# Adding attention masks with the row maximum instead of with matrix products

## What is computed

```python
# block 1, heads 0..3 (pairs of maps): causal
s = where(kpos <= qpos, q @ k.T * scale, -inf); p = softmax(s)
pd = p[:, :, 0] - lam * p[:, :, 1]
# block 1, heads 4..7 (pairs): three dilated windows (128,1), (512,4), (2048,16), joined by
# their log-sum-exp, which is one softmax of the scores + log(count of windows that hold the key)
# block 2: forgetting attention (causal, + cum_log_f), latent attention (causal, with rope),
# sliding window with a linear penalty and a sink:
s = where(0 <= dist < 128, q @ k.T * scale - slope * dist, -1e30)
p = softmax(concat(s, sink))
# and stick-breaking attention, with no softmax
```

## Time and profile before

| | |
|---|---|
| median of 3 runs | 2500.44 us (2499.18 to 2501.18) |
| the profiled execution | 2499.24 us |
| its span, first to last instruction | 2497.5 us |
| TensorE products, busy | 2447.4 us, 98% |
| VectorE, busy | 1238.2 us, 50% |
| ScalarE, busy | 953.7 us, 38% |
| mean granted TensorE clock | 0.997 of full |

### The profile page before, as it was taken

How to read it: one execution, slowest core, us unless ns; L and a number is a source line. 1 busy time by engine, 2 the same in 40 slices (tenths; PEclk the granted TensorE clock), 3 DMA queues, 4 the chain that set the end, 5 groups by cost and what they waited for, 6 DMA issues and landing times.

```text
span 2497.5 us, 30086 instructions
## 1 busy us (share of the span) xinstructions
PE 2447.4 (98%) x11932; PEld 1953.0 (78%) x11932; DVE 1238.2 (50%) x2019; ACT 953.7 (38%) x1765; POOL 0.2 (0%) x4
## 2 busy tenths in 40 slices
PE   8999999999999999999999999999999999999998
PEld 6888778887888778887767688888886767888887
DVE  6677553345577663344454463333355445433334
ACT  5355432223345542223456432212245554322222
POOL 0000000000000000000000000000000000000000
PEclk9999999999999999999999999999999999999999
DMA  4333223332333223333121123333322112333332
GB/s 162 103 89 89 80 81 100 94 115 62 97 104 90 84 66 112 101 93 110 54 66 43 57 102 98 96 98 95 116 65 71 51 43 76 103 100 94 101 93 93
DMA packets 65643, 221.46 MB, mean 89 GB/s; under 512 B 9056, under 2 KB 9696, under 8 KB 64736
## 3 DMA queue, kind: packets, MB, share of 16 engines
q1 hardware_dynamic: 65360, 219.28, 29.1%
q10 hardware_dynamic: 144, 0.26, 0.0%
HBM read 205.88 MB, written 2.10 MB: 83 GB/s over the span
## 4 chain that ended last, share of the span: by engine, by line
PE 92%; DVE 3%; ACT 2%; DMA 1%; issue 1%; SPq 0%; DVEq 0%; ACTq 0%
PE bank L452 26%; PE bank L454 26%; PE bank L453 25%; PE bank L1008 2%; PE bank L1607 1%; PE bank L1648 1%; PE bank L995 1%; PE bank L978 1%; DMA raw_w<-w_dram 1%; PE bank L1632 1%; PE bank L975 1%; DVE w_lo L860 1%; PE bank L1671 1%; PE bank L983 1%; PE bank L392 1%
## 5 line engine op out<-in xcount | busy, mean ns | idle before, releaser
L452 PE MATMUL bank<-h_hi,w_hi 128*128 128x512 f32 x2000 | 802.0, 401 | 3.5 <-ACT ks L1824 2.3
L454 PE MATMUL bank<-h_lo,w_hi 128*128 128x512 f32 x2000 | 780.8, 390 | 0.0
L453 PE MATMUL bank<-h_hi,w_lo 128*128 128x512 f32 x2000 | 779.3, 390 | 0.0
L860 DVE TENSOR_TENSOR w_lo<-raw_w,w_hi 128x1024 fp32r<-128x1024 f32 x360 | 433.2, 1221 | 208.0 <-ACT w_hi L852 204.0
L852 ACT ACTIVATE w_hi<-raw_w 128x1024 fp32r<-128x1024 f32 x360 | 376.9, 1056 | 321.3 <-DMA raw_w<-w_dram 321.2
L452 PEld LDWEIGHTS bank<-h_hi,w_hi 128*128 128x128 f32 x2000 | 375.7, 188 | 93.8 <-issue 21.3
L454 PEld LDWEIGHTS bank<-h_lo,w_hi 128*128 128x128 f32 x2000 | 375.4, 188 | 81.0
L453 PEld LDWEIGHTS bank<-h_hi,w_lo 128*128 128x128 f32 x2000 | 376.2, 188 | 71.9 <-issue 0.2
L452 PE MATMUL bank<-w_hi,act_hi 128*128 128x512 f32 x480 | 189.5, 395 | 3.1 <-DVE w_lo L860 3.1
L454 PE MATMUL bank<-w_lo,act_hi 128*128 128x512 f32 x480 | 187.0, 389 | 0.0
L453 PE MATMUL bank<-w_hi,act_lo 128*128 128x512 f32 x480 | 186.9, 389 | 0.0
(11 more groups left out here) (308 smaller groups left out, 2852.5 us busy)
## 6 DMA issues: line engine op xcount, KB each, us to landing
raw_w<-w_dram SPq DMA_DIRECT2D x360, 512.0 KB, 3.6
extra_raw<-w_dram SPq DMA_DIRECT2D x10, 512.0 KB, 5.0
ln_row<-row_dram SPq DMA_DIRECT2D x4, 1024.0 KB, 5.9
x<-x_dram SPq DMA_DIRECT2D x4, 512.0 KB, 6.8
rowp<-row_dram SPq DMA_DIRECT2D x2, 1024.0 KB, 10.3
rot_t<-raw_t SPq DMA_DIRECT2D x128, 16.0 KB
act_hi<-q_lo SPq DMA_DIRECT2D x16, 128.0 KB, 2.3
act_lo<-act_lo SPq DMA_DIRECT2D x16, 128.0 KB, 2.3
```

The source lines that it names most:

```text
L452: nc.tensor.matmul(dst, lh, rh, start=start, stop=False)
L453: nc.tensor.matmul(dst, ll, rh, start=False, stop=False)
L454: return nc.tensor.matmul(dst, lh, rl, start=False, stop=stop)
L860: nc.vector.tensor_tensor(lo_of(u), raw_of(u), hi_of(u).bitcast(F32), ALU.subtract) \
```

## The change

The maximum becomes one VectorE operation that adds the bank and an fp32 mask, multiplies by -1, writes the result over all `nk` columns into the probability buffer, and reduces it to its row minimum, which is the negated maximum (`masked_max`). The exponential then reads the probability buffer in place, with scale -1. The mask products are gone: L981, L983, L984, L1620, L1623; `SB` steps keep theirs (L1663). With this, the waits move: scores wait for `max_ready` instead of `probs_ready`, and the wait for `probs_normed` goes from the exponential to the maximum. The masks stay fp32: a causal mask of 512 columns of which VectorE clears the first 384, the log-count mask `mult`, and `swa`; they come in three transfers, and `m2_hi`, `m2_lo` and the rounding of `causal_r` and `swa_r` go. `sel_r` is rounded once, in place. Two query tiles of block 2 (`cq_t`) move to `mult` and to `vs0`.

```diff
+        causal = sb("causal", [P, SEQ])
+        mult = sb("mult", [P, SEQ])
+        swa = sb("swa", [P, 4, 2 * P])
...
+        def masked_max(bank, mask, to, low):
+            return nc.vector.tensor_tensor_reduce(out=to, in0=bank, in1=mask, scale=-1.0, scalar=3.0e38,
+                                                  op0=ALU.add, op1=ALU.min, accum_out=low)
...
-            sp.dma_start(masks[:, :], mask_in).then_inc(masks_loaded, 16)
+            sp.dma_start(causal[:, SEQ - P:SEQ], mask_in[:, M_CAUSAL:M_CAUSAL + P]).then_inc(masks_loaded, 16)
+            sp.dma_start(mult[:, :], mask_in[:, M_MULT:M_MULT + SEQ]).then_inc(masks_loaded, 16)
+            sp.dma_start(sbmask[:, :], mask_in[:, M_STRICT:M_STRICT + P]).then_inc(masks_loaded, 16)
...
 (block 1, scores)
                     if u and bank is S:
-                        pe.wait_ge(probs_ready, at(probs_ready, u - 1 + m))
+                        pe.wait_ge(max_ready, at(max_ready, u - 1 + m))
...
-                    nc.tensor.matmul(bank[m][:, 0:nk], q_two[i][m][rows, block_q], k_lo[i][rows, 0:nk], start=False, stop=False)
-                for m in range(2):
-                    if a < N_A:
-                        last = nc.tensor.matmul(bank[m][:, nk - P:nk], ident_r[:, :], causal_r[:, :], start=False, stop=True)
-                    else:
-                        nc.tensor.matmul(bank[m][:, 0:nk], ident_r[:, :], m2_hi[:, SEQ - nk:SEQ], start=False, stop=False)
-                        last = nc.tensor.matmul(bank[m][:, 0:nk], ident_r[:, :], m2_lo[:, SEQ - nk:SEQ],
-                                                start=False, stop=True)
-                    last.then_inc(scores_ready, 1)
+                    nc.tensor.matmul(bank[m][:, 0:nk], q_two[i][m][rows, block_q], k_lo[i][rows, 0:nk], start=False, stop=True) \
+                      .then_inc(scores_ready, 1)
...
 (block 1, exponential)
-                if u >= 2:
-                    act.wait_ge(probs_normed, at(probs_normed, 4 * a + qb))
-                nc.scalar.activation(prob[m][:, 0:nk], banks1(a, qb)[m][:, 0:nk], ACT.Exp,
+                nc.scalar.activation(prob[m][:, 0:nk], prob[m][:, 0:nk], ACT.Exp, scale=-1.0,
...
 (block 1, row_max)
-                nc.vector.tensor_reduce(small[:, 24 + 2 * qb + m:25 + 2 * qb + m], banks1(a, qb)[m][:, 0:(qb + 1) * P], AX.X,
-                                        ALU.max, negate=True).then_inc(max_ready, 1)
+                if u >= 2:
+                    dve.wait_ge(probs_normed, at(probs_normed, 4 * a + qb))
+                masked_max(banks1(a, qb)[m][:, 0:nk], (causal if a < N_A else mult)[:, SEQ - nk:SEQ], prob[m][:, 0:nk],
+                           small[:, 24 + 2 * qb + m:25 + 2 * qb + m]).then_inc(max_ready, 1)
...
 (block 2, scores; the waits for the banks change as in block 1)
-                for m in range(2):
-                    if kind == SWA:
-                        last = nc.tensor.matmul(S[m][:, 0:nk], ident_r[:, :], swa_r[:, head_of(a, m), 2 * P - nk:2 * P],
-                                                start=False, stop=True)
-                    else:
-                        last = nc.tensor.matmul(S[m][:, nk - P:nk], ident_r[:, :], causal_r[:, :], start=False, stop=True)
-                    last.then_inc(scores_ready, 1)
...
 (block 2, row_max)
+                if u >= 2:
+                    dve.wait_ge(probs_normed, at(probs_normed, u // 2 - (KIND[a] == FOX and not is_sb(NB * a + qb - 1))))
+                if (a, qb) == (SB0 + 2, 0):
+                    dve.wait_ge(sb_sp, at(sb_sp, TOTAL2["sb_sp"]))
+                elif (a, qb) == (SB0 + 2, 1):
+                    dve.wait_ge(sb_cum, at(sb_cum, TOTAL2["sb_cum"]))
+                mask = swa[:, head_of(a, m), 2 * P - nk:2 * P] if KIND[a] == SWA else causal[:, SEQ - nk:SEQ]
+                top_ = masked_max(banks(a, qb)[m][:, 0:nk], mask, probs_at(a, qb)[m][:, 0:nk], nm)
```

More of the change, by code:

```diff
@@ L172, in program @@
         ident_r = sb("ident_r", [P, P], F32R)
[L173 to L178, removed]
+        sbmask = sb("sbmask", [P, P])
+        sbmask_r = sb("sbmask_r", [P, P], F32R, at=addr["sbmask"])
+        causal = sb("causal", [P, SEQ])
+        mult = sb("mult", [P, SEQ])
+        swa = sb("swa", [P, 4, 2 * P])
         cos = sb("cos", [P, SEQ])
@@ L201, in program @@
         ytmp = sb("ytmp", [P, SEQ])
-        masks = sb("masks", [P, M_WIDTH], at=addr["pT0"])
-        rot_t = [sb(f"rot_t{i}", [P, SEQ], at=addr["swa_r"] + 4 * SEQ * i) for i in range(2)]
+        rot_t = [sb(f"rot_t{i}", [P, SEQ], at=addr["swa"] + 4 * SEQ * i) for i in range(2)]
         hn = [sb(f"hn{tb}", [P, D], at=shared + 4 * D * (tb % 2) + 16 * D * (tb // 2)) for tb in range(NB)]
@@ L225, in program @@
         ckv_t = sb("ckv_t", [P, SEQ], at=rowp_at + 12 * SEQ)
-        cq_t = [sb(f"cq_t{i}", [P, SEQ], at=m2_at + 4 * SEQ * i) for i in range(2)]
+        cq_t = [sb(f"cq_t{i}", [P, SEQ], at=addr[name]) for i, name in enumerate(("mult", "vs0"))]
         qr_t = sb("qr_t", [P, SEQ], at=addr["act_hi"] + 11 * 4 * SEQ)
@@ L231, in program @@
         TOK = ps[2:6]
-        sel_r = sb("sel_r", [P, 4 * P], F32R, at=addr["m2_lo"])
+        sel_r = sb("sel_r", [P, 4 * P], F32R, at=addr["const"] + 4 * C_SEL)
         cum_r = sb("cum_r", [P, SEQ], F32R, at=addr["ext2"])
@@ L318, in program @@
         sb_prob = sem("sb_prob")
-        swa_ready = sem("swa_ready")
         sq_parts = sem("sq_parts")
@@ L1361, in vector_block1 @@
                 st(nc.vector.tensor_copy(ident_r[:, :], ident))
[L1362 to L1367, removed]
+                st.wait(st(nc.vector.memset(causal[:, 0:SEQ - P], 0.0)))
+                st(nc.vector.tensor_copy(sel_r[:, :], const[:, C_SEL:C_SEL + 4 * P]))
+                dve.wait_ge(masks_loaded, 48)
+                st(nc.vector.tensor_copy(sbmask_r[:, :], sbmask[:, :]))
             for tb in range(NB):
@@ L1592, in bank_wait @@
                 elif a == N_ATT - 1:
-                    pe.wait_ge(probs_ready, at(probs_ready, u_of(*step_before(a, qb, 2), m) + 1))
+                    pe.wait_ge(max_ready, at(max_ready, u_of(*step_before(a, qb, 2), m) + 1))
                 elif a or qb:
-                    pe.wait_ge(probs_ready, at(probs_ready, u_of(*step_before(a, qb), m) + 1))
+                    pe.wait_ge(max_ready, at(max_ready, u_of(*step_before(a, qb), m) + 1))
             def scores(a, qb):
@@ L1606, in scores @@
                     rows = slice(HD * m, HD * m + HD)
-                    nc.tensor.matmul(S[m][:, 0:nk], q[rows, block_q], k[rows, k0:k1], start=True, stop=False)
+                    last = nc.tensor.matmul(S[m][:, 0:nk], q[rows, block_q], k[rows, k0:k1], start=True, stop=(kind == SWA))
+                    if kind == SWA:
+                        last.then_inc(scores_ready, 1)
                 for m in range(2):
@@ L1611, in scores @@
                         nc.tensor.matmul(S[m][:, 0:nk], sel_r[:, h * P:(h + 1) * P], cum_r[:, 0:nk],
-                                         start=False, stop=False)
+                                         start=False, stop=True).then_inc(scores_ready, 1)
                     elif kind == MLA:
@@ L1615, in scores @@
                         r = slice(r0, r0 + 32)
-                        nc.tensor.matmul(S[m][:, 0:nk], qr_t[r, block_q], z_t[r, 0:nk], start=False, stop=False,
-                                         tile_position=(r0, 0))
-                for m in range(2):
-                    if kind == SWA:
-                        last = nc.tensor.matmul(S[m][:, 0:nk], ident_r[:, :], swa_r[:, head_of(a, m), 2 * P - nk:2 * P],
-                                                start=False, stop=True)
-                    else:
-                        last = nc.tensor.matmul(S[m][:, nk - P:nk], ident_r[:, :], causal_r[:, :], start=False, stop=True)
-                    last.then_inc(scores_ready, 1)
+                        nc.tensor.matmul(S[m][:, 0:nk], qr_t[r, block_q], z_t[r, 0:nk], start=False, stop=True,
+                                         tile_position=(r0, 0)).then_inc(scores_ready, 1)
             def probs_transpose(a, qb, m):
@@ L1855, in softmax_exp @@
                 act.wait_ge(max_ready, at(max_ready, u + 1))
[L1856 to L1860, removed]
                 if KIND[a] == SWA:
@@ L1863, in softmax_exp @@
                     st(nc.scalar.activation(small[:, 44 + m:45 + m], sink, ACT.Exp, bias=small[:, 24 + c:25 + c]))
-                nc.scalar.activation(probs_at(a, qb)[m][:, 0:nk], banks(a, qb)[m][:, 0:nk], ACT.Exp, bias=small[:, 24 + c:25 + c],
+                nc.scalar.activation(probs_at(a, qb)[m][:, 0:nk], probs_at(a, qb)[m][:, 0:nk], ACT.Exp, scale=-1.0, bias=small[:, 24 + c:25 + c],
                                      accum_out=small[:, 32 + c:33 + c]).then_inc(probs_ready, 1)
```

16 lines of the change are left out of this document (6 added, 10 removed).

## The result

The changed kernel takes **2464.81 us** in the median (2463.91 to 2467.08, 4 runs), against 2499.81 us (2497.52 to 2501.18, 4 runs) for the kernel before on the same chip: a ratio of 0.9862, 95% interval 0.9845 to 0.9879. It is faster by 35 us. The forecast was 2463 us. The profiled execution took 2463.91 us with a span of 2462.1; the forecast for it was 2461.4.

A forecast was written before the change was run, and what follows sets the result against it. TensorE was taken to bound the kernel: 48.4 - 10.2 (chain losses) - 1.0 (clock) + 0.6 (banks) = 37.8 us off the profiled 2499.24, giving 2461.4, or 2463 us as median; 8-in-10 range 2450 to 2480.

The forecast's parts named there:

- The gross gain: 288 mask products removed from TensorE in blocks 1 and 2, priced by start-to-start intervals: 51.4 us, the upper end.
- only the columns come back: Rival: small products' cost beside columns is a switch their successor inherits; 28.5 us gross, 2483 us total; chance 0.10.
- Inherited cost: At 112 removed groups, the product behind takes over 0.03 us each: 3 us off, leaving 48.4.
- The new operation: VectorE's 224 combined maxima: 0.08 us longer each, 19 us in all, hidden except in chains where TensorE waits.
- Half speed: Rival: VectorE's combined maximum runs at half speed per element, adding 71 us to VectorE; 2478 us total; chance 0.10.
- A fixed cost: Rival: each combined maximum carries a fixed cost and VectorE becomes the bound; a loss from 1.06 us longer; chance 0.04.
- Block 1's ends: End of block 1's attention, each layer: removed 1.9 us lost, longer maxima add 0.5, 0.3 goes: 2.1 us a layer.
- the clock falls at the chain-bound ends too: Rival: four more clock falls of some 4 us, 2 us each: 2471 us, inside the forecast's range, chance included in 0.74.
- Block 2's last head: TensorE waits for late VectorE: 1.3 us removed is lost, 0.7 for longer maxima, 2.0 a layer; clock 1 us besides.
- Block 2's earlier waits: Two waits, for probabilities and a tile copy: 0.8 us lost plus 0.2 of lengthening, 1.0 us a layer.
- The banks' release: Score banks come free at the maximum instead of the exponential, so TensorE's bank waits go: 0.6 us gained.

The follow-up runs named there:

- the useless products: Changed kernel plus 24 products of 512 columns whose results go unused, issued in the waits of block 1's attention end: 2461.37 us, ratio 0.9849.

## Why the prediction was right, and where its terms were off

**Right: what bounds the kernel and where the gain is lost.** The products' time came back in the steps, was lost at the chains' ends, and with the products put back it went. 37.8 us were forecast on the profiled execution and 35.3 came. That it is so close is in part luck: terms that were too small by 5.6 us stand against terms that were too large by 3.2.

**The gross gain.** 51.4 us of intervals was the right measure, and "only the columns come back" is refuted: two 128-column products gave back 0.23 us a group in the steps, where their columns alone, at 0.2266 us per 512, are 0.11. By the estimate from the Trainium skill, "TensorE: Matmul & The Clock Gate", section on the back-to-back issue gap, that pair would also be 0.11 us; the traces side with the intervals.

**Inherited cost: about right, but a wait was missed.** I took off 0.03 us a group. The steps of block 1 saved 25.7 us of 29.1, 3.4 us less instead of the 1.7 charged for 57 groups. Of this, 31 causal groups lost 0.05 us each (8.6 removed, 7.0 saved) and 24 of the other mask 0.01 (19.4 and 19.1): 1.9 us. The kernel without masks saves 26.0 us on the same 55 groups, where the kernel after saves 26.1, so this part lies in the products and not in VectorE's operation. The other 1.5 us stand at one group in each layer. That step, the first of the last pair, starts 3.5 us behind the step before it, where some 8.5 are usual, and TensorE now waits in it for a tile copy, which it didn't before:

```profile
320.69 1.25 PE L1007 MATMUL bank<-pT,vs 128*64 128x128 f32 x12 [0.73 <-ACT pT L1209]
```

I had read the slack of one usual step only, and this one isn't usual.

**The new operation: over-priced.** I took 0.08 us longer each, 19 us of VectorE. Its busy time grew by 2.7, and with the 2.4 us of mask preparation that went counted in by some 5, since the accumulator read runs beside the next operation. The duration was right (689 ns for 686), the read was there (83), and the sum of durations was the wrong measure for VectorE, as I had said it was for TensorE. Half speed is refuted by that row. The sentence of the Trainium skill's "Vector Engine (DVE) Microarchitecture Reference", "Points that are easy to get wrong", is about two SBUF sources that aren't bf16. The traces have a fused operation with that pairing, without an accumulator, and it isn't halved either, 691 ns against 686 with a bank; no run has it with one:

```profile
L1398 DVE SCALAR_TENSOR_TENSOR rope_a<-rope_a,sz 128x512 f32<-128x512 f32 x4 | 2.8, 691 | 0.1
```

A fixed cost is refuted by the timeline, and the experiment with 83 us more on VectorE shows what it would have done: 22 us, at the ends and in block 2. Before it became a loss, the operation would have had to be more than 0.37 us longer; how much more, no run shows.

**Block 1's ends: the failed step.** "Block 1's end had no such fall, and its waits grow by 2 us. I put 1 us on it." The clock fell at both ends, 0.50 for 7 us each, and by the useless products that cost 1.3 us a layer, 2.7 in all. The rest of the loss was of the size that I had put: with the clock at 1.00, the kernel with the useless products lost 2.5 us a layer in this stretch (0.2 saved of 5.2), where 2.2 was charged. The waits grew by 1.7 us a layer, about the 2 us that I had put: those for the tile copy from 4.0 to 6.3 us over the two layers, and 1.0 for the normalised probabilities; 0.73 a layer of it is the wait just shown. With the clock's cost on top, the ends gave -2.5 us where 0.8 was forecast. (The table has my 1 us for the clock at the last heads; put here, the forecast would be -0.2.) This was the rival "the clock falls at the chain-bound ends too", with two new falls instead of four and 1.3 us each instead of 2.

**Block 2's last head: over-priced.** I charged 2.0 us a layer and the clock there; 4.2 us were removed and 1.7 saved, a loss of 2.5 us for both layers instead of 5.4. The longer pairs of maxima (0.7 a layer) didn't exist, and the clock's fall in layer 1 was absent from this execution. That is luck of the execution, worth 0.9 us: the second profile of the same kernel has a fall of 6.8 us there and saves 0.9 us less in layer 1, and has a fall of 3.4 us instead of 6.8 in layer 2 and saves 0.7 more. The wait for the probabilities grew from 3.07 to 3.41 us only; behind it one for a tile copy, 0.25 us before, became 1.09.

**Block 2's earlier waits** lost 2.7 us where 3.0 was forecast. **The banks' release** was worth nothing that the medians show; the 0.6 us that I put on it are too few for them to confirm or refute.

The too small terms (1.7 in block 1's steps, 3.3 at its ends, 0.6 in the rest) outweigh the too large ones (2.9 and 0.3 in block 2) by 2.4 us, which is what lies between the table's 37.7 and 35.3.

## What to carry to other kernels

Work taken from a saturated engine comes back stretch by stretch: here 93% of it in 55 steady steps of block 1, and less than nothing where the engine already waited for a chain that didn't change. So list the chain-bound ends first, and every step that follows its predecessor sooner than usual, charge them with the whole of what is removed there, and ask whether the longer wait also brings the clock down. Then look for work that doesn't depend on the chain and can be issued inside it; enough of it must be found for the whole chain, since moving a piece of cover here only moved the wait.

## What the runs showed of the hardware

- The granted clock fell to 0.50 behind waits of 0.49 and 1.66 us that lie close together (332.7 to 335.6 us), and stood at 1.00 in the old kernel behind one of 1.52. The kernel with its products put back, whose order there is the old one's, lost 1.8 us in that stretch of layer 1 and 0.3 in layer 2's, and its clock fell in layer 1 alone, for 3.4 us; its stretch in columns as above:

```profile
354.00:356.00 2.00, 2.00 (x10) 1.57 (x8) 1.05 (x1) 0.55 (x1) 0.00 (x0) 0.50 0.00 0
```

- A VectorE operation with an accumulator read of 83 ns behind it starts its successor 0.61 us after itself at 512 columns, although it is shown with 0.68: durations of both overlap.
- ScalarE's exponential is 0.03 us longer from SBUF than from the bank (718 and 689 ns at 512 columns), and its accumulator read 0.01 shorter (188 and 198).
